# Hybrid decoder trunk, two layers: the combine with a 0/1 operand in float32r, pair weights moved into the copies, and the turn of the expert outputs over eight PSUM banks

## The reference, cut to what matters

```python
comb = (g_onehot[..., None] * comb_in[:, :, None, :])     # (token, group, expert): two nonzero weights per token
hh = silu(xn @ w_gate[e]) * (xn @ w_up[e]) * comb[token, e]
y  = sum over experts e of hh @ w_down[e]                 # 32 experts, hidden width 256
x  = x + y
x  = x + sigmoid(RMSNorm(x) @ W_pg) * (p[i] @ W_ple)      # what comes next
```

## Time and profile before

| | us |
|---|---|
| median of 3 executions | 1317.95 |
| lowest, highest | 1312.43, 1317.98 |
| the profiled execution, its own time | 1314.42 |
| its span, from the first to the last instruction | 1312.7 |
| PE busy in the span | 1153.6 (88%) |
| DVE busy | 557.1 (42%) |
| ACT busy | 366.5 (28%) |
| POOL busy | 154.1 (12%) |

### The profile page before, as it was taken

One profiled execution on the slowest core, in us unless ns is written; L12 is line 12 of the kernel. 1 busy time (PEld: TensorE's weight loads), 2 busy tenths in 40 slices (PEclk: granted clock), 3 DMA queues, 4 the chain that ended last, 5 costly groups with the idle time before them and its releaser, 6 DMA issues.

```text
span 1312.7 us, 21119 instructions
## 1 busy us (share of the span) xinstructions
PE 1153.6 (88%) x7828; PEld 901.7 (69%) x7828; DVE 557.1 (42%) x1111; ACT 366.5 (28%) x619; POOL 154.1 (12%) x174
## 2 busy tenths in 40 slices
PE   5998879998689998888899978899995999888897
PEld 5985879888555554446889668898884555444597
DVE  3569885335531111113546889553346111111234
ACT  4332343223212221112344124332232122111232
POOL 0112321001000100000102142101000101000001
PEclk9999999999889999999979989999997999999997
DMA  5523853544369999991525258344524999999512
GB/s 160 143 84 117 336 178 109 179 146 145 129 239 418 417 417 418 419 373 55 177 71 171 79 198 310 113 145 147 174 97 179 383 417 417 418 417 417 202 65 80
DMA packets 136280, 300.49 MB, mean 229 GB/s; under 512 B 12656, under 2 KB 101616, under 8 KB 119792
## 3 DMA queue, kind: packets, MB, share of 16 engines
q1 hardware_dynamic: 136176, 299.18, 61.6%
HBM read 298.11 MB, written 1.05 MB: 228 GB/s over the span
## 4 chain that ended last, share of the span: by engine, by line
PE 51%; DVE 15%; DMA 14%; SPq 9%; issue 5%; ACT 3%; POOL 1%; POOLq 0%; ACTq 0%; DVEq 0%
PE ps L650 48%; SPq L524 8%; DMA gu_ring<-in_w_exp_up_dram 7%; DVE work L1568 6%; DMA ring<-in_w_in_dram 4%; PE ps L653 3%; DVE wsplit L1473 2%; DMA ring<-in_w_exp_up_dram 2%; ACT wsplit L1066 1%; DVE work L1499 1%; DMA ring<-in_w_out_b_dram 1%; ACT work L1066 1%; DVE ps L1550 0%; DMA work<-in_positions_dram 0%; DVE mx L1553 0%
## 5 line engine op out<-in xcount | busy, mean ns | idle before, releaser
L650 PE MATMUL ps<-h_pair,wsplit 128*128 128x256 f32 x3264 | 424.3, 292 | 31.1 <-ACT wsplit L1066 24.9
L650 PEld LDWEIGHTS ps<-h_pair,wsplit 128*128 128x128 f32 x3264 | 412.3, 199 | 41.7 <-issue 38.9
L1473 DVE TENSOR_TENSOR wsplit<-ring,wsplit 128x1024 fp32r<-128x1024 f32 x136 | 171.1, 1263 | 169.2 <-ACT wsplit L1066 160.9
L1066 ACT ACTIVATE wsplit<-ring 128x1024 fp32r<-128x1024 f32 x136 | 139.2, 1053 | 232.9 <-DMA ring<-in_w_in_dram 146.8
L650 PE MATMUL ps<-gu_ring,hT 128*64 128x256 f32 x1280 | 159.1, 391 | 29.4 <-DMA gu_ring<-in_w_exp_up_dram 20.3
L650 PEld LDWEIGHTS ps<-gu_ring,hT 128*64 128x64 f32 x1280 | 90.5, 139 | 98.7 <-issue 33.8
L650 PE MATMUL ps<-work,ring 128*128 128x256 f32 (+2 forms) x640 | 143.0, 380 | 2.6 <-DMA ring<-in_w_out_b_dram 2.2
L1066 ACT ACTIVATE work<-ps 128x512 f32 (+5 forms) x132 | 73.2, 558 | 241.3 <-PE ps L653 171.2
L650 PEld LDWEIGHTS ps<-work,ring 128*128 128x128 f32 (+2 forms) x640 | 111.5, 177 | 30.1 <-issue 3.9
L1796 DVE TENSOR_TENSOR pT<-pT,ps 128x128 f32<-128x128 f32 x64 | 18.4, 288 | 267.3 <-ACT pT L1228 267.3
L1568 DVE SCALAR_TENSOR_TENSOR work<-work,convT 128x256 f32<-128x256 f32 x240 | 114.1, 545 | 0.2
(11 more groups left out here) (181 smaller groups left out, 893.9 us busy)
## 6 DMA issues: line engine op xcount, KB each, us to landing
ring<-in_w_in_dram SPq DMA_DIRECT2D x52, 1024.0 KB, 5.3
gu_ring<-in_w_exp_gate_dram SPq DMA_DIRECT2D x40, 1024.0 KB, 20.7
gu_ring<-in_w_exp_up_dram SPq DMA_DIRECT2D x40, 1024.0 KB, 22.0
down_ring<-in_w_exp_down_dram SPq DMA_DIRECT2D x40, 1024.0 KB, 21.9
lent_down<-in_w_exp_down_dram SPq DMA_DIRECT2D x24, 1024.0 KB, 22.1
ring<-in_w_exp_gate_dram SPq DMA_DIRECT2D x12, 1024.0 KB, 19.7
ring<-in_w_exp_up_dram SPq DMA_DIRECT2D x12, 1024.0 KB, 20.5
lent_gate_up<-in_w_exp_gate_dram SPq DMA_DIRECT2D x12, 1024.0 KB, 20.4
```

The source lines that it names most:

```text
L650: return nc.tensor.matmul(o, lhsT, rhs, start=first, stop=last)
L1066: return nc.scalar.activation(o, i, ACT.Copy)
L1473: TT(tile_split[:, m, 1, :, :], tile_of(name, m), tile_split[:, m, 0, :, :].bitcast(F32), ALU.subtract).then_inc(tile_low, 1)
```

## The change

The moving operand of the combine becomes `selT`, which is 1.0 where the turned weights are above zero and else 0.0, in float32r. The pair weight of a slot, `slot_weight` (a sum of the turned weights over the tokens), is multiplied in when the turned expert outputs leave PSUM. These are written in two parts, both float32r: ACT writes the rounded product into `y_tok[0]`, and DVE writes the product less that part into `y_tok[1]`, which lies in `wsplit`. The combine runs one float32r matmul for each part, 64 in all. `work_r` is the same memory as `work`, seen as float32r.

The turn of `ys` goes over all eight banks in the order of `TURN_BANKS`, first all slot blocks of the first half of the channels, then those of the second. Every bank is read by both ACT and DVE. PE turns `gw` within the last step of `experts`, ahead of the last `turn_out`. The units `cb0` and `cb1` wait for the first four DVE results, `cb2` and `cb3` for all eight.

```diff
--- before.py
+++ after.py
@@ -95,6 +95,7 @@
 UI = {u: i for i, u in enumerate(UNITS)}
 NU = len(UNITS)
 BANKS = 3
+TURN_BANKS = [0, 1, 2, 3, 6, 7, 4, 5]
 TAPS_BEFORE = [50, 13, 13]
 
 
@@ -186,6 +187,9 @@
         starts = sb("starts", [1, WIDE * NE], I32)
         most = sb("most", [1, 1], I32)
         mx = sb("mx", [P, 2, 2, 3])
+        with ExitStack() as rounded:
+
+            work_r = rounded.enter_context(nc.sbuf_tensor("work_r", [P, 12928], F32R))
         work = sb("work", [P, 12928])
         ps = ctx.enter_context(nc.psum_tensor("ps", [P, 8, 512], F32))
 
@@ -255,8 +259,11 @@
         pflat = pT[:, :, :].rearrange("p a n -> p (a n)")
         hh = pflat[:, 0:2 * P].rearrange("p (b n) -> p b n", b=2)
         sg = pflat[:, 2 * P:4 * P].rearrange("p (b n) -> p b n", b=2)
-        y_tok = area(4608, 4, D)
-        gwT = area(11776, 4, S)
+        y_tok = [work_r[:, 4608:4608 + 4 * D].rearrange("p (s d) -> p s d", s=4),
+                 wsplit[:, :, :, :, :].rearrange("p m i g n -> p (m i g n)").rearrange("p (s d) -> p s d", s=4)]
+        selT = work_r[:, 11776:11776 + 4 * S].rearrange("p (s n) -> p s n", s=4)
+        slot_part = area(12800, TC, 4)
+        slot_weight = area(12808, 4)
         route_at = [10240]
 
         def rt(n):
@@ -393,7 +400,9 @@
         gwT_psum = lsem("gwT_psum")
         gwT_ready = lsem("gwT_ready")
         ytok_psum = lsem("ytok_psum")
-        ytok_read = [lsem("ytok_read_act"), lsem("ytok_read_dve")]
+        slot_summed = lsem("slot_summed")
+        ytok_high = lsem("ytok_high")
+        ytok_low = lsem("ytok_low")
         pT_tr = lsem("pT_tr")
         p_ready = lsem("p_ready")
         psig_ready = lsem("psig_ready")
@@ -920,6 +929,13 @@
                                       sel[:, t, :], t + part == 0, t + part == TC)
                     last.then_inc(gather_psum, 1)
 
+                def turn_weights():
+                    pe.wait_ge(gw_ready, 2)
+                    for t in range(TC):
+                        for s in range(4):
+                            last = tr(ps[:, 4 + t, s * P:(s + 1) * P], gw[:, t, s * P:(s + 1) * P])
+                        last.then_inc(gwT_psum, 1)
+
                 def experts(per):
                     def gate_up(it, k, part):
 
@@ -975,6 +991,8 @@
                         two_before = k >= 2
                         if not ending:
                             gate_up(it, k, 0)
+                        if k == (PEEL + BODY) * per + 1:
+                            turn_weights()
                         if two_before:
                             turn_out(it, k - 2)
                         if one_before:
@@ -995,32 +1013,24 @@
                     experts(1)
 
 
-                pe.wait_ge(gw_ready, 2)
-                for t in range(TC):
-                    for s in range(4):
-                        b = 4 + t
-                        last = tr(ps[:, b, s * P:(s + 1) * P], gw[:, t, s * P:(s + 1) * P])
-                    last.then_inc(gwT_psum, 1)
-                for s in range(4):
-                    for half in range(2):
-                        i = 2 * s + half
-                        if i == 0:
-
-                            wait_last_ys(pe, most_pe, windows, ys_ready)
-                        if i >= 2:
-                            pe.wait_ge(ytok_read[i % 2], (i - 2) // 2 + 1)
-                        for j in range(4):
-                            last = tr(ps[:, 6 + i % 2, j * P:(j + 1) * P], ys[:, half * 4 + j, s * P:(s + 1) * P])
-                        last.then_inc(ytok_psum, 1)
-                pe.wait_ge(gwT_ready, 2)
-                pe.wait_ge(ytok_read[0], 4)
-                pe.wait_ge(ytok_read[1], 4)
+                for i, b in enumerate(TURN_BANKS):
+                    half, s = i // 4, i % 4
+                    if i == 0:
+
+                        wait_last_ys(pe, most_pe, windows, ys_ready)
+                    if b in (4, 5):
+                        pe.wait_ge(gwT_ready, b - 3)
+                    for j in range(4):
+                        last = tr(ps[:, b, j * P:(j + 1) * P], ys[:, half * 4 + j, s * P:(s + 1) * P])
+                    last.then_inc(ytok_psum, 1)
                 for m in range(4):
                     free_bank(f"cb{m}")
+                    pe.wait_ge(ytok_low, 4 + 4 * (m // 2))
                     for j in range(2):
                         for s in range(4):
-                            last = mm(two(bank(f"cb{m}"))[:, j, :], y_tok[:, s, (2 * m + j) * P:(2 * m + j + 1) * P],
-                                      gwT[:, s, :], s == 0, s == 3)
+                            for part in range(2):
+                                last = mm(two(bank(f"cb{m}"))[:, j, :], y_tok[part][:, s, (2 * m + j) * P:(2 * m + j + 1) * P],
+                                          selT[:, s, :], s + part == 0, s + part == 4)
                     last.then_inc(unit_ready, 1)
 
 
@@ -1259,11 +1269,16 @@
                     experts(WIDE)
                 with act.Else():
                     experts(1)
-                for i in (0, 2, 4, 6):
+                act.wait_ge(slot_summed, 1)
+                for i, b in enumerate(TURN_BANKS):
+                    half, s = i // 4, i % 4
                     act.wait_ge(ytok_psum, i + 1)
-                    copy(y_tok[:, i // 2, 0:512], ps[:, 6, :]).then_inc(ytok_read[0], 1)
+                    nc.scalar.activation(y_tok[0][:, s, half * 512:(half + 1) * 512], ps[:, b, :], ACT.Copy,
+                                         scale=slot_weight[:, s:s + 1]).then_inc(ytok_high, 1)
                 act.wait_ge(pT_tr, 1)
                 copy(pT[:, :, :], two(ps[:, 7, :])).then_inc(p_ready, 1)
+
+                wait_unit(act, l, "cb3")
                 high_tiles(l, "pg0")
                 squares("ple", sq_p, xT, [f"cb{m}" for m in range(4)])
                 for m in range(4):
@@ -1817,10 +1832,18 @@
                     experts(1)
                 for t in range(TC):
                     dve.wait_ge(gwT_psum, t + 1)
-                    nc.vector.tensor_copy(gwT[:, :, t * P:(t + 1) * P], ps[:, 4 + t, :].rearrange("p (s n) -> p s n", s=4)).then_inc(gwT_ready, 1)
-                for i in (1, 3, 5, 7):
-                    dve.wait_ge(ytok_psum, i + 1)
-                    nc.vector.tensor_copy(y_tok[:, i // 2, 512:1024], ps[:, 7, :]).then_inc(ytok_read[1], 1)
+                    turned = ps[:, 4 + t, :].rearrange("p (s n) -> p s n", s=4)
+                    TS(selT[:, :, t * P:(t + 1) * P], turned, 0.0, None, ALU.is_gt)
+                    nc.vector.reduce_sum(slot_part[:, t, :], turned, AX.X).then_inc(gwT_ready, 1)
+                dve.wait_ge(gwT_ready, 2)
+                TT(slot_weight, slot_part[:, 0, :], slot_part[:, 1, :], ALU.add).then_inc(slot_summed, 1)
+                dve.wait_ge(slot_summed, 1)
+                for i, b in enumerate(TURN_BANKS):
+                    half, s = i // 4, i % 4
+                    at = slice(half * 512, (half + 1) * 512)
+                    dve.wait_ge(ytok_high, i + 1)
+                    STT(y_tok[1][:, s, at], ps[:, b, :], slot_weight[:, s:s + 1], y_tok[0][:, s, at].bitcast(F32),
+                        ALU.mult, ALU.subtract).then_inc(ytok_low, 1)
                 for m in range(4):
                     add_to_x(f"cb{m}", m)
                     wait_evacuated(dve, f"cb{m}")
```

## The result

| | before | changed |
|---|---|---|
| median, us | 1317.97 (4 runs, 1312.43 to 1320.03) | 1297.84 (4 runs, 1295.48 to 1301.48) |
| the profiled execution, us | 1314.42 | 1295.48 |
| its span, us | 1312.7 | 1293.7 |

The ratio is 0.988, with a 95% interval of 0.985 to 0.9911. It is an estimate from the runs and not the quotient of the two medians, which is 0.9847: by the ratio the gain is 15.8 us, by the medians 20.1. Run again in the experiments, on one chip beside the kernel before, the changed kernel had a median of 1296.78 us against 1314.38, a ratio of 0.9862 (0.9839 to 0.9885). The forecast was 1300 in a range of 1293 to 1309. On each of the two chips of the experiments one execution of the kernel before was in a slower state (1365.3 and 1492.47 us); it doesn't enter the ratios.

A forecast was written before the change was run, and what follows sets the result against it. PE held 51% of the span, but stages had different limits, so the change was priced in its own: 1.9 us (turn) plus 6.05 (combine), 7.95 per layer, 15.9 in all, off a mean of 1315.7, said as 1300, range 1293 to 1309.

The forecast's parts named there:

- The weight turn, moved: Eight transposes of `gw` moved ahead of the last `turn_out`, into a PE gap of 0.8 to 0.9 us; cost 0 to 0.2, taken as 0.
- DVE's work before the copies: Two comparisons, two sums and a small sum before the scaled copies end at about 597.25 us; ACT's added wait is 0.03 us.
- The copies: Turn of `ys`: ACT's scaled copies step 0.58 us, DVE's subtractions 0.66; DVE-bound, `cb0` starts 1.9 us earlier.
- The combine: 64 float32r matmuls at 0.1225 us take 7.84 us instead of 13.9: 6.05 us less per layer.
- The lower price of the prediction: Combine: half of the gather's step at full clock, 0.11 us a matmul and 7.0 us, the low end of its price.
- The second half under the first: Last four DVE operations lie under `cb0` and `cb1`, with 1.2 us to spare before `cb2`; `p` turns 7.95 us earlier per layer.
- What comes behind: Stages after the combine: weights of `pg0` lie ready, loads move along, no new transfer collision; the whole gain passes through.
- The sum: Both layers together: 2 x 7.95 = 15.9 us gained, forecast time 1300 us.
- (a): Rival, copies of the turn: ACT and DVE don't overlap, 1.5 us a tile; 3.4 us gained per layer, time 1309; chance 0.06.
- (c): Rival, combine: weight loads of 190 ns set the step, so float32r gains nothing; only 1.9 us left, 1312; chance 0.03.
- (d): Rival, combine: runs at the gather's 0.343 us a matmul, 21.9 us; 6.1 us slower per layer, 1328; chance 0.02.
- (b): Rival: clock falls to 1.2 GHz for the whole combine, 15.7 us; gain 0.1 per layer, time 1315.5; chance 0.03.

## Why the prediction was right, point by point

- **The weight turn, moved, costs nothing.** Right. PE turned `gw` from 590.89 to 591.98 in its wait for ACT, and the turn of `ys` starts 4.68 us after the last down product, where it was 4.63. That it had to move was not argued in the prediction: left behind, it costs 1.1 us and risks the clock.
- **DVE's work before the copies.** Right. Comparison 0.69 (0.69 was the nearest row), sum 0.68 (0.66 extrapolated from the earlier trace rows), small sum 0.16, its end at 594.26; ACT started at 594.45, released by PE. The wait for `slot_summed` cost nothing, with 0.1 us to spare.
- **The copies.** Right. The steps are (4.74 - 0.69) / 7 = 0.58 and (5.36 - 0.75) / 7 = 0.66, the values of the earlier trace rows. The combine starts 4.68 us after ACT's last piece has ended, and 4.7 was forecast.
- **The combine.** Right, with a small error in size: 7.64 us (598.12 to 605.76), not 7.84, and 0.119 us a matmul, not 0.1225. In the second run of the same kernel it is 0.121. Part of the error is the division: 17.64 / 144 = 0.1225 has the drain of the last matmul in it. Without its 0.28 us the row gives 17.36 / 143 = 0.1214, and 64 of these are 7.77 us; the second run had 7.76. The lower price of the prediction, 0.11 and 7.0 us, is 0.6 us too low: no run came under 0.119.
- **The second half under the first.** Right: no wait between `cb1` and `cb2`, and 2.6 us if it is taken away. What the prediction didn't say is that the same order guards the clock.
- **What comes behind.** Right in sum: the stretch from the turn of `p` in layer 0 to the last down product of layer 1 took 613.8 us before and 614.1 after, and the end of the program 57.1 in both. In the changed kernel `pg0` ran partly at the 1.2 GHz level in both layers (7.48 and 7.50 us), before only in layer 1. So not every stage was as long as before: this one was 1.5 us longer in layer 0, and that the sum grew by 0.3 us alone is the luck of other pieces that were shorter in this execution.
- **The sum.** 15.9 us forecast, 16.4 by the stages, 19.0 in the profiled execution and 20.1 between the first medians. The ratio gives 15.8. The excess over the stages is in the front of layer 0 in the profiled execution and was not traced in the medians. That the forecast of 1300 and the measured 1297.84 lie within 2.2 us of each other owes something to this scatter, too; the stages are the sharper test.
- **The rivals.** (a) is out: ACT and DVE ran at their own steps. (c) and (d) are out by the step of 0.119. (b) didn't occur here, but it was under-argued: the prediction found it unlikely since the turn before had gaps too and kept its clock. The experiments show how near it lay. With PE's pause at 0.71 us, the clock stayed; at 1.86 it fell in one layer of two; at 3.35 it fell in both, for 1.6 us each and not the 7.9 that the rival priced. With several waits in the turn (two banks) it fell in both layers too.

## What to carry to other kernels

Price a float32r form by a row with the same columns and weights in the same trace, and the copies by their steps, not their durations: here that gave each term to within 0.2 us. When a tile leaves PSUM through two engines, count the banks before the passes: the half-priced combine was worth 2.1 to 2.8 us per layer with two banks, and 5.2 with eight (22.05 to 16.87). And when PE waits in front of a dense stretch, add what the clock may take behind the wait to the wait itself; other matmuls in the pause were cheaper than the pause.

## What the runs showed of the hardware that was not expected

- The 1.2 GHz level after a pause can cost about half as much again as the pause: 1.6 us behind 3.35 us of idle PE, and 24 float32r matmuls that fill the pause take that away.
- Float32r matmuls of 256 columns, each with a new weight tile, came every 0.119 to 0.121 us in the combine and every 0.1214 in the projections (17.64 less a last drain of 0.28, over 143), at clock 1.00, against 0.434 for a float32 one (two records of 0.217).
